# The second block's recurrence at 128 query columns a level, with two PSUM banks and four masked copies for each of its levels

## What is computed

```python
def step(S, inp):                       # a chunk of tokens at a time
    q, k, v, lf = inp
    b = jnp.cumsum(lf, axis=2)          # running sum of the log forget gates
    inter = jnp.einsum('bhte,bhev->bhtv', q * jnp.exp(b), S)
    diff = b[:, :, :, None, :] - b[:, :, None, :, :]
    D = jnp.exp(jnp.where(causal[None, None, :, :, None], diff, NEG_BIG))
    A = jnp.einsum('bhtse,bhse->bhts', q[:, :, :, None, :] * D, k)
    intra = jnp.einsum('bhts,bhsv->bhtv', A, v)
    ...
    return S_new, inter + intra
```

## Time and profile before

| | |
|---|---|
| median of 3 runs | 2545.63 us (2545.42 to 2548.38) |
| the profiled execution | 2537.04 us, span of its instructions 2535.3 us |
| TensorE busy | 2301.1 us (91%) |
| VectorE, ScalarE, GpSimd busy | 1099.8 (43%), 712.9 (28%), 33.9 us (1%) |
| mean granted TensorE clock | 0.943 of full |
| the two mixings' units | from about 1610 to 1780 and from 2160 to 2325 us |

### The profile page before, as it was taken

One profiled execution on the slowest core, in us unless ns is written; L12 is line 12 of the kernel. 1 busy time (PEld: TensorE's weight loads), 2 busy tenths in 40 slices (PEclk: granted clock), 3 DMA queues, 4 the chain that ended last, 5 costly groups with the idle time before them and its releaser, 6 DMA issues. The chain is left out here.

```text
span 2535.3 us, 36274 instructions
## 1 busy us (share of the span) xinstructions
PE 2301.1 (91%) x14950; PEld 1676.8 (66%) x14950; DVE 1099.8 (43%) x1656; ACT 712.9 (28%) x912; POOL 33.9 (1%) x31
## 2 busy tenths in 40 slices
PE   6966776999999999999999799999999999999998
PEld 4635765443333333433333699988999999988998
DVE  4546444121111111211112666666755655767654
ACT  3332122111100000110111444535433433536332
POOL 0001110000000000000000000000000000000000
PEclk8967898999999999999999799999999999999999
DMA  9630025899999999999997555532555555533651
GB/s 370 239 152 1 1 67 214 333 416 417 417 417 417 417 417 416 417 417 417 417 408 282 173 182 184 166 117 84 184 184 182 182 181 184 154 96 120 196 183 67
DMA packets 236123, 626.61 MB, mean 247 GB/s; under 512 B 13144, under 2 KB 153976, under 8 KB 200056
## 3 DMA queue, kind: packets, MB, share of 16 engines
q1 hardware_dynamic: 232808, 622.12, 65.4%
q10 hardware_dynamic: 3216, 3.06, 0.4%
HBM read 624.10 MB, written 1.05 MB: 247 GB/s over the span
## 5 line engine op out<-in xcount | busy, mean ns | idle before, releaser
L1841 DVE TENSOR_TENSOR w_low<-ring,w_high 128x2048 fp32r<-128x2048 f32 x168 | 383.9, 2289 | 279.7 <-ACT w_high L1836 279.7
L1836 ACT ACTIVATE w_high<-ring 128x2048 fp32r<-128x2048 f32 x168 | 320.0, 1910 | 274.9 <-PE bank L2051 138.6
L1597 PE MATMUL bank<-ring,ut 128*64 128x512 f32 x1024 | 255.7, 653 | 60.0 <-DMA ring<-in_exp_w_dram 59.7
L1597 PEld LDWEIGHTS bank<-ring,ut 128*64 128x64 f32 x1024 | 74.3, 149 | 225.7 <-issue 128.9
L1568 PE MATMUL bank<-ring,xt 128*64 128x512 f32 x1024 | 223.3, 594 | 0.3 <-ACT xt L1651 0.3
L1568 PE MATMUL bank<-ring_odd,xt 128*64 128x512 f32 x1024 | 223.3, 594 | 0.0
L2066 PE MATMUL bank<-h_high,w_high 128*128 128x256 f32 x1408 | 188.4, 283 | 15.2 <-ACT h_high L1939 15.2
L2066 PEld LDWEIGHTS bank<-h_high,w_high 128*128 128x128 f32 x1408 | 176.9, 189 | 16.0 <-ACT h_high L1939 15.8
L2066 PE MATMUL bank<-h_high,w_low 128*128 128x256 f32 x1408 | 187.1, 282 | 0.0
L2066 PE MATMUL bank<-h_low,w_high 128*128 128x256 f32 x1408 | 187.0, 282 | 0.0
L2066 PEld LDWEIGHTS bank<-h_high,w_low 128*128 128x128 f32 x1408 | 176.4, 189 | 0.0
(11 more groups left out here) (531 smaller groups left out, 3057.4 us busy)
## 6 DMA issues: line engine op xcount, KB each, us to landing
ring<-in_exp_w_dram SPq DMA_DIRECT2D x256, 1024.0 KB, 22.5
ring_odd<-in_exp_w_dram SPq DMA_DIRECT2D x128, 1024.0 KB, 21.6
ring<-in_ffn_w_gate_dram SPq DMA_DIRECT2D x44, 1024.0 KB, 5.4
ring<-in_ffn_w_up_dram SPq DMA_DIRECT2D x44, 1024.0 KB, 5.4
ring<-in_ffn_w_down_dram SPq DMA_DIRECT2D x44, 1024.0 KB, 4.9
ring<-in_w_in_dram SPq DMA_DIRECT2D x36, 1024.0 KB, 5.4
ring<-in_ada_w_dram SPq DMA_DIRECT2D x24, 1024.0 KB, 12.7
ring<-in_w_out_dram SPq DMA_DIRECT2D x8, 1024.0 KB, 5.2
```

The source lines that it names most:

```text
L1597: ins = nc.tensor.matmul(bank[2 + dh][64 * dh:64 * dh + 64, :], ut[:, r % 4, 64 * (r // 4):64 * (r // 4) + 64], w[:, x, 512 * dh:512 * dh ...
L1836: nc.scalar.activation(w_bufs[0][u % BUFS], ring2[:, u % RING2, :], ACT.Copy).then_inc(high2, 1)
L1841: nc.vector.tensor_tensor(w_bufs[1][u % BUFS], ring2[:, u % RING2, :], w_bufs[0][u % BUFS].bitcast(F32), ALU.subtract).then_inc(low2, 1)
```

## The change

The levels from 1 on take all 128 query columns instead of the 64 that can hold valid pairs; the mask alone picks them. The masks grow from 576 to 1024 columns. Each level fills two banks, one for heads 0 and 1 and one for 2 and 3, as level 0 did. Since every level now uses both banks, TensorE's level n waits for the copies of level n-1, the first pair of heads before head 0, the second before head 2. VectorE copies each level by four instructions of 256 elements, one for a head, each over the blocks 0 and 2 of its head. `cross` waits for the copies of level 7. A has 3 blocks for a head in place of 4, and GpSimd clears all of them (1536 columns instead of 1024).

```diff
     for b in (1, 2, 4, 8, 16, 32, 64):
-        later = i[i % (2 * b) >= b]
-        levels.append((i[:, None] // (2 * b) == later[None] // (2 * b)) & (i[:, None] % (2 * b) < b))
+        levels.append((i[:, None] // (2 * b) == i[None] // (2 * b)) & (i[None] % (2 * b) >= b) & (i[:, None] % (2 * b) < b))
...
-        levels = prods[:, 0:LEVEL_COLS]
+        levels = prods[:, 0:NLEV * P]
-        level_masks = sb("level_masks", [P, LEVEL_COLS], U8)
+        level_masks = sb("level_masks", [P, NLEV, P], U8)
...
-        at_ = hT[:, :, :].rearrange("p c t -> p (c t)").rearrange("p (h b t) -> p h b t", h=4, b=4)
-        on_diagonal = hT[:, :, :].rearrange("p c (two t) -> p c two t", two=2)[:, :, 0, :]
+        at_ = hT[:, 2:8, :].rearrange("p c t -> p (c t)").rearrange("p (h b t) -> p h b t", h=4, b=3)
...
-                nc.gpsimd.memset(on_diagonal, 0.0).then_inc(sem(f + "cleared"), 1)
+                nc.gpsimd.memset(at_[:, :, :, :], 0.0).then_inc(sem(f + "cleared"), 1)
...
-                    if n == 0:
-                        for h in range(4):
-                            for a in range(TT):
-                                at = P * (2 * (h % 2) + a)
-                                ins = nc.tensor.matmul(bk[6 + h // 2][:, at:at + P], kr[:, h, P * a:P * a + P], qp[:, h, P * a:P * a + P],
-                                                       start=True, stop=True)
-                            if h % 2:
-                                ins.then_inc(sem(f + "level_ready"), 1)
-                    else:
-                        pe.wait_ge(sem(f + "masked_in"), max(2, n))
-                        for h in range(4):
-                            for a in range(TT):
-                                at = P // 2 * (2 * h + a)
-                                later = qp[:, h, P * a:P * a + P].rearrange("p (k two b) -> p k two b", two=2, b=2 ** (n - 1))[:, :, 1, :]
-                                ins = nc.tensor.matmul(bk[6 + n % 2][:, at:at + P // 2], kr[:, h, P * a:P * a + P], later, start=True, stop=True)
-                        ins.then_inc(sem(f + "level_ready"), 1)
+                    for h in range(4):
+                        if n and h % 2 == 0:
+                            pe.wait_ge(sem(f + "masked_in"), 2 * (n - 1) + h // 2 + 1)
+                        for a in range(TT):
+                            at = P * (2 * (h % 2) + a)
+                            ins = nc.tensor.matmul(bk[6 + h // 2][:, at:at + P], kr[:, h, P * a:P * a + P], qp[:, h, P * a:P * a + P],
+                                                   start=True, stop=True)
+                        if h % 2:
+                            ins.then_inc(sem(f + "level_ready"), 1)
 
                 def cross():
                     pe.wait_ge(sem(f + "factors"), NLEV)
-                    pe.wait_ge(sem(f + "masked_in"), NLEV)
+                    pe.wait_ge(sem(f + "masked_in"), 2 * NLEV)
...
                 def level(n):
-                    dve.wait_ge(sem(f + "level_ready"), n + 2)
+                    dve.wait_ge(sem(f + "level_ready"), 2 * n + 2)
...
-                    if n == 0:
-                        for j in range(2):
-                            st.tell(nc.vector.copy_predicated(on_diagonal[:, 4 * j:4 * j + 4, :], level_masks[:, 0:P].unsqueeze(1).to_broadcast([P, 4, P]),
-                                                              bk[6 + j][:, :].rearrange("p (c t) -> p c t", c=4)), f + "masked_in")
-                    else:
-                        b = 2 ** (n - 1)
-                        at = P + P // 2 * (n - 1)
-                        mask = level_masks[:, at:at + P // 2].rearrange("p (k b) -> p k b", b=b).unsqueeze(1).to_broadcast([P, DC, P // (2 * b), b])
-                        later = on_diagonal.rearrange("p c (k two b) -> p c k two b", two=2, b=b)[:, :, :, 1, :]
-                        st.tell(nc.vector.copy_predicated(later, mask, bk[6 + n % 2][:, :].rearrange("p (c k b) -> p c k b", c=DC, b=b)), f + "masked_in")
+                    for j in range(2):
+                        blocks = at_[:, 2 * j:2 * j + 2, :, :].rearrange("p h b t -> p (h b) t")
+                        for h in range(2):
+                            ins = nc.vector.copy_predicated(blocks[:, 3 * h:3 * h + 3:2, :], level_masks[:, n:n + 1, :].to_broadcast([P, 2, P]),
+                                                            bk[6 + j][:, T * h:T * h + T].rearrange("p (a t) -> p a t", a=2))
+                        st.tell(ins, f + "masked_in")
...
-                nc.vector.tensor_copy(level_masks[:, :], levels)
+                nc.vector.tensor_copy(flat(level_masks[:, :, :]), levels)
```

More of the change, by code:

```diff
@@ L158 @@
 NLEV = 8
-LEVEL_COLS = P + (NLEV - 1) * P // 2
 ROWS_A = [("emb_ln_g", 8), ("emb_ln_b", 8), ("ada_b", 48), ("q_norm_g", 2), ("kv_norm_g", 1), ("mla_out_g", 4),
@@ L2596, in level @@
                         st.step(nc.vector.tensor_tensor(k4[:, :, 0, :], k4[:, :, 0, :], halves[:, :, 1:2].to_broadcast([P, blocks, b]), ALU.mult), f + "factors")
-                    if n == 0:
-                        for j in range(2):
-                            st.tell(nc.vector.copy_predicated(on_diagonal[:, 4 * j:4 * j + 4, :], level_masks[:, 0:P].unsqueeze(1).to_broadcast([P, 4, P]),
-                                                              bk[6 + j][:, :].rearrange("p (c t) -> p c t", c=4)), f + "masked_in")
-                    else:
-                        b = 2 ** (n - 1)
-                        at = P + P // 2 * (n - 1)
-                        mask = level_masks[:, at:at + P // 2].rearrange("p (k b) -> p k b", b=b).unsqueeze(1).to_broadcast([P, DC, P // (2 * b), b])
-                        later = on_diagonal.rearrange("p c (k two b) -> p c k two b", two=2, b=b)[:, :, :, 1, :]
-                        st.tell(nc.vector.copy_predicated(later, mask, bk[6 + n % 2][:, :].rearrange("p (c k b) -> p c k b", c=DC, b=b)), f + "masked_in")
+                    for j in range(2):
[4 more added lines that the diff above has]
+                        st.tell(ins, f + "masked_in")
                 def take_cross():
-                    dve.wait_ge(sem(f + "level_ready"), NLEV + 2)
-                    dve.wait_ge(sem(f + "masked_in"), NLEV + 1)
+                    dve.wait_ge(sem(f + "level_ready"), 2 * NLEV + 1)
+                    dve.wait_ge(sem(f + "masked_in"), 2 * NLEV)
                     st.tell(nc.vector.tensor_copy(at_[:, :, 1, :], bk[6][:, :].rearrange("p (h t) -> p h t", h=4)), f + "at_ready")
```

## The result

| | kernel before | changed kernel |
|---|---|---|
| median of the runs compared (us) | 2545.53 (2539.92 to 2548.38, 6 runs) | 2520.86 (2517.03 to 2531.7, 6 runs) |
| ratio, 95% interval | | 0.9918 (0.9897 to 0.994) |
| the profiled execution (us) | 2537.04 | 2519.73 |
| its span (us), mean granted clock | 2535.3, 0.943 | 2517.9, 0.952 |

The forecast was 2548.2, +2.6 us. The changed kernel came out 25 us faster in these runs. Over the whole study the 26 runs of the changed kernel have a mean of 2530.8 us, and the 76 runs of the one before that stand beside the later experiments one of 2539.5: 8.7 us, 0.34%. (With its 14 other runs, these six and the eight of `before_again`, the kernel before has a mean of 2539.9.) Without the six runs of the table the changed kernel is 6.1 us faster, with an interval of 2.9 to either side.

A forecast was written before the change was run, and what follows sets the result against it. TensorE was taken to bound the kernel. A layer cost -0.51 + 0.58 + 1.09 = +1.16 us, two layers +2.3, the masks' cast +0.3: +2.6 on 2545.63 gave 2548.2 us, with a range from 2542 to 2553.5.

The forecast's parts named there:

- TensorE's columns, 0: Levels from 1 on, TensorE: doubling 64 columns to 128 costs 0, since both take 107 ns a record.
- Rival 3: Levels on TensorE: columns cost what the skill's gap formula says, +8.6 us in all, 2554.2 us; chance 0.05.
- The copies: VectorE, each level: a 256-element copy takes 0.46 us, 0.36 to its successor, all four 1.54 us.
- Rival 4: VectorE's copies: one of 256 costs as much as one of 512, +8.3 us, 2553.9 us; chance 0.05.
- The wait at `cross`: TensorE stalls 1.52 us for level 7's copies; 1.09 us of it reach the mixing's end.
- Level 1: TensorE starts after level 0's first pair of copies, 0.51 us sooner a layer, with no second wait.
- The cast, +0.3: Cast of the larger masks, ahead of TensorE's 4.43 us wait for a weight part: grows by 0 to 0.35 us.
- The sum of these, +2.6: Two layers' waits, +1.16 us each or +2.3, with the masks' cast +0.3; chance 0.60.
- The clock: Granted clock around the waits at level 1, unit 10 and `cross`: no net change taken.
- rival 1: Clock improves: level 1's fall and both falls before unit 10 are gone, -3.5 us, 2542.1 us; chance 0.12.
- rival 2: New idle time ahead of `cross` pulls the clock down in both layers, +5.7 us, 2551.3 us; chance 0.10.
- The base: Sum set on 2545.63 us, the median of the runs shown, 8.6 us above the profiled execution.

The follow-up runs named there:

- before_again: The kernel before, unchanged, run and profiled once more; 2539.71 us (8 runs), ratio 0.9991.
- half_cols: The changed kernel with 64 columns in the levels from 1 on, the recurrence's values left out of the levels; 2532.85 us in one run.
- old_place: The changed kernel with all other tensors kept where they were, but for the recurrence's two outputs; 2535.3 us (12 runs), ratio 0.9984.
- after_128_cross: The changed kernel with 128 bytes more behind its masks and `cross` waiting for level 7's first pair of copies only; 2518.4 us (6 runs), ratio 0.9928.
- pad_masks: The kernel before with only the mask buffer enlarged, 1024 bytes a partition instead of 576; 2532.88 us (12 runs), ratio 0.9981.
- both_64: The kernel before with 64 bytes ahead of the second block's weight and activation buffers, so both move together; 2545.33 us in one run.

## Why the prediction was wrong, and where it was right

**TensorE's columns, 0: right.** A level of 128 columns takes 1.70 us, one of 64 in `half_cols` does too. The gap formula that the Trainium skill gives in "TensorE: Matmul & The Clock Gate", section "Back-to-back issue gap", would have put 26.7 ns on each record; no trace here has them between 64 and 128 columns. Rival 3 falls.

**The copies: right, a little dear.** 0.434 us instead of 0.46, and 1.44 for four instead of 1.54. Rival 4 falls. The wait at `cross` was 1.40 and 1.39 us in the two layers (forecast 1.4 to 1.5), at level 3 0.42 and 0.63 (0.5), `hgrn_values` idled 0.47 and 0.68 (at most 0.5 was forecast), levels 2 and 4 to 7 waited for nothing. One new wait wasn't foreseen: behind unit 10 TensorE waits 0.39 us for `u_low`, which stands on VectorE behind level 5's copies (0.2 in `old_place`); the prediction took 0 for what is queued there. ScalarE's 0.43 us of slack was used up as foretold. The way to the end of the mixing was not quite the one forecast: the prediction sent the wait at `cross` through TensorE's `turn(5)` and ScalarE, but in `after_128_cross` a wait 0.86 us shorter takes only some 0.3 us off the end, so most of the delay comes by VectorE's copies. The size came out right all the same (see the sum below).

**Level 1: right.** In the changed kernel the wait shrank by 0.2 us only, 0.5 were forecast. But the moved tensors by themselves lengthen it: `pad_masks` waits 3.10 us. With the tensors in the same place it went from 2.74 to 2.18 in `old_place`, and from 3.10 to 2.54 in the changed kernel, 0.56 us each time.

**The cast, +0.3: right.** 4.68 us in `old_place` against 4.43, +0.25; the rest of the changed kernel's 4.9 comes with the moved tensors.

**The sum of these, +2.6: borne out.** `old_place` has exactly these parts and next to nothing moved: +1.4 ± 1.7 us at equal clock, an interval that holds 2.6 and 0 alike. Its trace is sharper. From level 0 to the first product of the recurrence's output it takes 109.74 and 108.12 us in the two mixings, the kernel before 111.39 and 108.42. The clock is half for 3.4 and 0 us of it, before for 10.2 and 3.4; taken off at 0.44 of that time (worked out in the paragraph on the clock), the mixings are 1.3 and 1.2 us longer, where 1.16 was forecast.

**The clock: this step failed in size, and it was left at 0 against a row that spoke for more.** The prediction saw that the 1.5 us wait before unit 10 lost the clock behind 64-column matmuls and that as long a wait behind 256-column ones lost nothing, and said that the idle time alone doesn't decide. Yet it took "no net change", and gave the improvement, rival 1, 0.12. All falls at unit 10 went, as rival 1 said. Level 1's did not: they remain in 12 of 14 mixings, ten of them 3.4 us long, where with 64 columns there were 24 in 26 mixings, 14 of them 6.8. And rival 2 holds in part: 5 of the 14 mixings with 128 columns have a fall of 3.4 us at the new wait ahead of `cross`, and two more have one at the wait of 1.7 us ahead of the recurrence's output product; none of the 26 with 64 has either. Together a mixing spends 5.1 us at half clock instead of 8.1 (means over all traces). A fall of 6.8 us costs 3.0 us and one of 3.4 costs 1.5, 0.44 of the time at half clock: 2 x (8.1 - 5.1) x 0.44 = 2.6 us a run, gained. With +2.6 that is nothing. This gain is worked out from the traces; in the times it can't be told from the clock's chance.

**The tensors' places: this is the step that failed, a term put at nothing without a reason.** Under "Elsewhere" the sum took the larger mask buffer for its cast and its DMA, +0.3 and 0, and no step asked what lies behind it in SBUF. Moving those by 448 bytes made 8,064 matmuls 0.89 ns faster: -7.2 us, nearly three times all that was reckoned, shown by `pad_masks` alone. +2.6 - 2.6 - 7.2 = -7.2 us; the means of the runs give -8.7, and -6.1 ± 2.9 without the first six. At equal clock, where the clock's term drops out, the parts measured one by one, -6.9 by `pad_masks` and +1.4 by `old_place`, make -5.5, and the 26 runs of the whole change make -6.0.

**The base: 16 of the first 25 us are chance.** The prediction set its sum on 2545.63, 8.6 us above the profiled execution, "for a reason that the profile doesn't show". The likely reason is the granted clock, of the first block above all, which differs between executions of one kernel: the kernel before ranged from 2525.4 to 2550.4 us over 76 runs. The three runs shown lay near the top of that (11 of the 76 reach 2545.4), and five of the six runs of the changed kernel below all 20 later ones. The clock of those three runs isn't known. For the six it is, and it carries 10 of the 16 us: at equal clock they are 7.4 us faster than the kernel before, by their times 17.5. Against the base of all runs, 2539.5, the forecast would have been 2542.1; measured, 2530.8. It stays wrong by 11 us, and by the sign.

## What to carry to other kernels

A change that resizes a buffer moves all that is allocated behind it. Where thousands of matmuls depend on those tensors, test the shift by itself, old code with the new size and new code with the old places, before crediting the change; here it was worth 7 us, and another place, found by trial, some 20, more than the whole change. Where runs go with the granted clock, compare them at equal clock, or over so many runs that both sides have seen the same range. And when a wait costs the clock, look at what TensorE did ahead of it: columns that take no time of their own kept it up at one wait here, though not at another.

## What the chip showed that I had not expected

- Back-to-back matmuls of 128 x 128 weights by 256 columns, at full clock and without a wait, run at 113.3 to 120.0 ns each, and which paces occur goes with how far apart moving and stationary operands lie in SBUF. `both_64` shows that the distance counts; which property of it, and why, is open.
- One distance can have two paces: 113.3 and 117.8 ns at 192 and at 64, 118.7 and 120.0 at 128, 160 and 384. A pace holds as long as the row of matmuls isn't broken, for the greater part of a SwiGLU in these traces, and may be the other one behind a wait or a stretch of other work; the same kernel picks differently in another execution.
- Levels of 64 and of 128 columns take the same 1.70 us, but only behind the 64-column ones did the wait of 1.5 us ahead of unit 10 bring the clock down, in 21 of 26 mixings against 0 of 14.
- The same kernel's first block loses between executions some 10 us more or less to the granted clock, most of it by whether the clock stays at half for 55 us from about 140 us on (15 of 20 traces) or not. The profile shows no cause.
